# Decode attention inside a hybrid decoder step: three PSUM banks shared by turned keys and probabilities, and the splits of the value pages in another order

## The reference

```python
k_past = cache_k[l][page_table].reshape(n_dec, PAST_LEN, DA_HEADS, 2 * DA_HEAD_DIM)
v_past = cache_v[l][page_table].reshape(n_dec, PAST_LEN, DA_HEADS, DA_V_DIM)
k_all = jnp.concatenate([k_past, ka], axis=1)
v_all = jnp.concatenate([v_past, va], axis=1)
oa = diff_attention(qa, k_all, v_all, q_pos_s, k_pos_s, lam)

s = jnp.einsum('bqhmd,bkhmd->bhmqk', q, k) * (DA_HEAD_DIM ** -0.5)
p = jax.nn.softmax(s + bias, axis=-1)
a = p[:, :, 0] - lam * p[:, :, 1]
return jnp.einsum('bhqk,bkhd->bqhd', a, v)
```

## Time and profile before

| what | value |
|---|---|
| time, median of 3 runs | 1933.44 us (1932.71 to 1934.54) |
| time of the profiled execution | 1933.36 us |
| its span, first to last instruction | 1931.1 us |
| mean granted TensorE clock | 0.964 |
| PE busy over the span | 1776.0 us (92%) |
| DVE, ACT, POOL busy | 780.2 us (40%), 661.2 us (34%), 97.2 us (5%) |
| PE share of the chain that ended last | 85%, of which line 297 is 68% |

### The profile page before, as it was taken

How to read it: one execution, slowest core, us unless ns; L and a number is a source line. 1 busy time by engine, 2 the same in 40 slices (tenths; PEclk the granted TensorE clock), 3 DMA queues, 4 the chain that set the end, 5 groups by cost and what they waited for, 6 DMA issues and landing times.

```text
span 1931.1 us, 32243 instructions
## 1 busy us (share of the span) xinstructions
PE 1776.0 (92%) x13095; PEld 1678.0 (87%) x13095; DVE 780.2 (40%) x1084; ACT 661.2 (34%) x867; POOL 97.2 (5%) x169
## 2 busy tenths in 40 slices
PE   5999999998998775989889999899999899999996
PEld 5999999987997545777768999779998799999996
DVE  2333332244223775776753222344344433333123
ACT  3333331124223554666753222123322433332111
POOL 0000000000002420000000000210000000000002
PEclk9999999999998898999989999999999999999998
DMA  4222222230430014787851232152222122222221
GB/s 140 88 88 88 89 88 93 82 101 30 134 124 33 1 39 147 260 281 269 278 178 45 86 102 85 46 184 88 88 87 87 34 89 88 88 88 84 85 98 46
DMA packets 146734, 204.09 MB, mean 106 GB/s; under 512 B 5538, under 2 KB 127330, under 8 KB 146658
## 3 DMA queue, kind: packets, MB, share of 16 engines
q1 hardware_dynamic: 145506, 198.55, 31.6%
q0 software_dynamic: 1152, 4.46, 0.6%
HBM read 191.59 MB, written 11.40 MB: 105 GB/s over the span
## 4 chain that ended last, share of the span: by engine, by line
PE 85%; DVE 6%; ACT 5%; issue 3%; DMA 0%; SPq 0%; POOL 0%; POOLq 0%; ACTq 0%; DVEq 0%
PE ps L297 68%; PE ps L1255 3%; PE ps L1280 2%; PE ps L1237 2%; PE ps L974 2%; DVE vp_lo L1377 2%; ACT vp_hi L1373 1%; PE ps L988 1%; ACT kt_hi L1355 1%; PE ps L614 1%; PE ps L1683 1%; PE ps L1675 1%; PE ps L1295 1%; PE ps L699 1%; DVE kt_lo L1356 1%
## 5 line engine op out<-in xcount | busy, mean ns | idle before, releaser
L297 PE MATMUL ps<-xh,w_hi_t 128*128 128x272 f32 x2432 | 512.1, 292 | 27.4 <-DVE xl L651 18.6
L297 PE MATMUL ps<-xl,w_hi_t 128*128 128x272 f32 x2432 | 506.4, 290 | 0.0
L297 PE MATMUL ps<-xh,w_lo_t 128*128 128x272 f32 x2432 | 505.8, 290 | 0.0
L283 DVE TENSOR_TENSOR w_lo_t<-w_raw,w_hi_t 128x2048 fp32r<-128x2048 f32 (+1 forms) x112 | 252.4, 2254 | 519.2 <-ACT w_hi_t L279 519.2
L297 PEld LDWEIGHTS ps<-xh,w_hi_t 128*128 128x128 f32 x2432 | 385.6, 191 | 32.5 <-issue 21.1
L297 PEld LDWEIGHTS ps<-xl,w_hi_t 128*128 128x128 f32 x2432 | 386.7, 191 | 0.0
L297 PEld LDWEIGHTS ps<-xh,w_lo_t 128*128 128x128 f32 x2432 | 384.6, 191 | 0.0
L279 ACT CAST w_hi_t<-w_raw 128x2048 fp32r<-128x2048 f32 (+1 forms) x112 | 209.9, 1874 | 277.5 <-PE ps L297 277.5
L297 PE MATMUL ps<-hh,w_hi_t 128*128 128x272 f32 x704 | 145.8, 288 | 0.0
L297 PE MATMUL ps<-hl,w_hi_t 128*128 128x272 f32 x704 | 145.3, 288 | 0.0
L297 PE MATMUL ps<-hh,w_lo_t 128*128 128x272 f32 x704 | 144.9, 287 | 0.0
(11 more groups left out here) (243 smaller groups left out, 2040.4 us busy)
## 6 DMA issues: line engine op xcount, KB each, us to landing
w_raw<-in_ffn_w_gu_dram SPq DMA_DIRECT2D x44, 1024.0 KB, 5.0
w_raw<-in_w_in_dram SPq DMA_DIRECT2D x32, 1024.0 KB, 5.6
k_page<-in_cache_k_dram SPq DMA_DIRECT2D x64, 512.0 KB, 4.2
v_page<-in_cache_v_dram SPq DMA_DIRECT2D x64, 512.0 KB, 4.7
w_raw<-in_ffn_w_down_dram SPq DMA_DIRECT2D x16, 1024.0 KB, 5.1
w_raw<-in_ffn_w_down_dram SPq DMA_DIRECT2D x8, 768.0 KB, 4.4
w_raw<-in_w_branch_a_dram SPq DMA_DIRECT2D x4, 1024.0 KB, 5.1
st_in<-in_state_ret_dram SPq DMA_DIRECT2D x8, 512.0 KB, 5.3
```

The lines of the kernel that those rows point to most:

```text
L283: nc.vector.tensor_tensor(w_lo_t[:, j, 0:nk], w_raw[:, j, 0:nk], w_hi_t[:, j, 0:nk].bitcast(F32), ALU.subtract).then_inc(lo_split, 1)
L297: mm = nc.tensor.matmul(ps[:, bank + half, 0:HALF], w[:, j, k, w_cols], m[:, k0 + k, half * HALF:half * HALF + HALF], start=start and k == ...
```

## The change

Two things change, both inside `DecodeAttention`. The number and kind of instructions stays the same.

First, the turned key halves and the turned probabilities now go round three banks, 0, 1 and 5, in the order in which PE makes them: two halves for each key page, and the probabilities of request b-1 behind key page 2 of request b. Each of them waits until the work three places back has been read by DVE. Before, a key half waited for the half two places back.

Second, ACT and DVE take the value pages in another place: pages 2 and 3 right behind key page 3, and page g right behind key page g for g = 4 to 7. On ACT, key page 2 also goes ahead of the copy of the last output rows (`act_keep`). The order on PE, on POOL and on SP does not change.

```diff
+                order = []
+                for b in range(DEC):
+                    for g in range(PAGES):
+                        order += [("k", b, g, half) for half in range(2)]
+                        if b and g == 2:
+                            order.append(("p", b - 1))
+                order.append(("p", DEC - 1))
+                self.order = order
+                self.place = {item: n for n, item in enumerate(order)}
+
+            def bank(self, *item):
+                return (0, 1, 5)[self.place[item] % 3]
+
+            def bank_free(self, pe, *item):
+                n = self.place[item] - 3
+                if n >= 0 and self.order[n][0] == "k":
+                    _, b, g, half = self.order[n]
+                    pe.wait_ge(self.kT_lo, 16 * b + 2 * g + half + 3)
+                elif n >= 0:
+                    pe.wait_ge(self.pT_lo, 2 * self.order[n][1] + 3)
...
-                    pe.wait_ge(self.kT_lo, 16 * b + 2 * g + half + 1)
+                    self.bank_free(pe, "k", b, g, half)
                     for h in range(4):
-                        mm = nc.tensor.transpose(ps[:, half, h * P:h * P + P],
+                        mm = nc.tensor.transpose(ps[:, self.bank("k", b, g, half), h * P:h * P + P],
...
                 pe.wait_ge(self.pT_lo, 2 * b + 2)
-
-                nc.tensor.matmul(ps[:, 5, 0:ROWS], p_s[:, 0:P], ident[:, 0:ROWS], start=True, stop=True)
+                self.bank_free(pe, "p", b)
+                bank = self.bank("p", b)
+
+                nc.tensor.matmul(ps[:, bank, 0:ROWS], p_s[:, 0:P], ident[:, 0:ROWS], start=True, stop=True)
...
+                self.act_key(act, b, 2)
                 if older:
                     self.act_keep(act, b - 2)
-                self.act_key(act, b, 2)
...
                 self.act_key(act, b, 3)
+                if past:
+                    self.act_value(act, b - 1, 2)
+                    self.act_value(act, b - 1, 3)
                 for g in range(4, PAGES):
+                    self.act_key(act, b, g)
                     if past:
-                        self.act_value(act, b - 1, g - 2)
-                    self.act_key(act, b, g)
-                if past:
-                    self.act_value(act, b - 1, 6)
-                    self.act_value(act, b - 1, 7)
+                        self.act_value(act, b - 1, g)
...
                 self.dve_key(dve, b, 3)
+                if past:
+                    self.dve_value(dve, b - 1, 2)
+                    self.dve_value(dve, b - 1, 3)
                 for g in range(4, PAGES):
+                    self.dve_key(dve, b, g)
                     if past:
-                        self.dve_value(dve, b - 1, g - 2)
-                    self.dve_key(dve, b, g)
-                    if past and g == 5:
-                        self.dve_weigh(dve, b - 1)
-                if past:
-                    self.dve_value(dve, b - 1, 6)
-                    self.dve_value(dve, b - 1, 7)
+                        self.dve_value(dve, b - 1, g)
+                        if g == 5:
+                            self.dve_weigh(dve, b - 1)
```

More of the change, by code:

```diff
@@ L1261, in turn_p @@
                 pe.wait_ge(self.pT_lo, 2 * b + 2)
-                nc.tensor.matmul(ps[:, 5, 0:ROWS], p_s[:, 0:P], ident[:, 0:ROWS], start=True, stop=True)
+                self.bank_free(pe, "p", b)
+                bank = self.bank("p", b)
+                nc.tensor.matmul(ps[:, bank, 0:ROWS], p_s[:, 0:P], ident[:, 0:ROWS], start=True, stop=True)
                 for g in range(1, PAGES):
-                    nc.tensor.transpose(ps[:, 5, ROWS * g:ROWS * g + ROWS], p_s[0:ROWS, P * g:P * g + P],
+                    nc.tensor.transpose(ps[:, bank, ROWS * g:ROWS * g + ROWS], p_s[0:ROWS, P * g:P * g + P],
                                         ident[0:ROWS, 0:ROWS])
@@ L1349, in key_half @@
             def key_half(self, b, g, half, hi):
-                src = ps[:, half, :].rearrange("p (h c) -> p h c", c=P)
+                src = ps[:, self.bank("k", b, g, half), :].rearrange("p (h c) -> p h c", c=P)
                 n = slice(P * (g % 2), P * (g % 2) + P)
@@ L1378, in dve_value, with p_parts @@
                                         ).then_inc(self.v_lo, 1)
-            def p_parts(self):
-                return ((ps[:, 5, :].rearrange("p (g c) -> p g c", c=ROWS), pT[:, 0:PAGES, 0:ROWS],
+            def p_parts(self, b):
+                return ((ps[:, self.bank("p", b), :].rearrange("p (g c) -> p g c", c=ROWS), pT[:, 0:PAGES, 0:ROWS],
                          pT[:, 0:PAGES, ROWS:P]),
@@ L1413, in act_p @@
                 act.wait_ge(self.o_done, b + 1)
-                for src, hi, _ in self.p_parts():
+                for src, hi, _ in self.p_parts(b):
                     nc.scalar.copy(hi, src).then_inc(self.pT_hi, 1)
@@ L1494, in dve_p @@
                 dve.wait_ge(self.pT_hi, 2 * b + 2)
-                for src, hi, lo in self.p_parts():
+                for src, hi, lo in self.p_parts(b):
                     nc.vector.tensor_tensor(lo, src, hi.bitcast(F32), ALU.subtract).then_inc(self.pT_lo, 1)
```

## The result

| | before | after |
|---|---|---|
| median | 1933.44 us (1932.07 to 1934.96, 9 runs) | 1938.55 us (1936.33 to 1946.55, 9 runs) |
| profiled execution, its span | 1933.36 us, 1931.1 us | 1936.33 us, 1934.1 us |
| mean granted clock | 0.964 | 0.962 |
| first turn to last merge | 283.04 us | 287.59 us |

The ratio is 1.003 (95% interval 1.0019 to 1.004): the change made the kernel about 5.1 us slower. The forecast was 1940.0 us, slower by 6.6. The profiled execution is the fastest of the nine runs of the changed kernel, so the trace shows somewhat less than the median: 4.55 us within the decode stage, 0.93 us ahead of it and -2.5 us behind it.

A forecast was written before the change was run, and what follows sets the result against it. The decode attention stage was taken as bound by PE, broken by short waits. Terms 5.7 - 1.2 - 3.5 + 5.6 = +6.6 us on 1933.36 gave 1940.0 us, with a range from 1928 to 1949 us.

The forecast's parts named there:

- pairs: Key pages (4, 5) and (6, 7), seven requests: value split waits for `values`, each score 0.41 us late; +5.7 us.
- front of a request: Key page 1 to second score, six requests: third bank removes a half-turn wait, about 0.2 us gained each; -1.2 us.
- request 0, front of request 1: Turns with no values between: waits shrink or move earlier, scores wait for one subtraction less; -3.5 us together.
- falls of the clock: Waits of about 1.8 us ahead of late scores: four of 14 followed by 1.2 GHz, about 1.4 us each; +5.6 us.
- the old share: Four of seven waits from 1.46 us up in the old trace were followed by 1.2 GHz; forecast took 2 in 7.
- The rival with a holding clock: Decode stage: the clock stays full behind the long waits; 1934.4 us, no change that can be told; chance 0.27.
- That DVE work hangs on ACT's row of copies, the same number as before: Second score of a request: low part of key page 3 follows ACT's copies, so only about 0.2 us is gained.
- the bound of -4.9: Request 0 and front of request 1: largest gain, if the low-clock score at 756.10 becomes a fast one.
- The late value page: Value page 4's load may land after ACT wants it: nothing taken, upper bound 0.4 x 7 = 2.8 us.
- The rival that the bank was the limit: Front of a request: gain reaches the second score, 1.26 us in each of six requests; 1928.0 us; chance 0.18.

The follow-up runs named there:

- the filled kernel: The changed kernel with 12 unread turns of the identity ahead of each third and fourth score of requests 1 to 7, 168 in all: 1933.36 us.
- The order alone: The changed kernel with two banks for key halves and bank 5 for the probabilities, as before, keeping the new ACT and DVE order: 1940.21 us.
- the ring alone: The changed kernel with its three banks, but ACT and DVE in the order of before the change: 1925.65 us.
- the paired order: The changed kernel, three banks, with ACT and DVE taking key pages 4 and 5, then value pages 4 and 5, likewise 6 and 7: 1916.16 us.
- the copy put back: The changed kernel with ACT's copy of the finished output ahead of key page 2 again: 1937.65 us.

## Why the prediction was right

The time came out near the forecast, and by the mechanism forecast. All four terms have the sign that was forecast. The pairs have the size too; the front of a request was mis-sized by a wrong step, request 0 came out 1.0 us beyond its term, and the falls came near theirs partly by luck. All of it is taken from the profiled executions.

| term | predicted | measured | how |
|---|---|---|---|
| pairs | +5.7 | +5.6 | 6 x (0.41 + 0.39), and 0.39 + 0.42 in request 1 |
| front of a request | -1.2 | -2.4 | 6 x (-0.60 + 0.11 + 0.09) |
| request 0, front of request 1 | -3.5 | -4.5 | -5.73 + 1.19 |
| falls of the clock | +5.6 | +6.0 | 1.53 + 1.58 + 1.63 + 0.67 + 0.63 |
| sum | +6.6 | +4.7 | the stage is 4.55 longer |

**The pairs: right.** A delay of 0.41 us was read from one row of PE, the end of `values`, and the new rows have 0.41 from turn to score in the first pair; in the second the score is 7.73 - 7.34 = 0.39 later. (The request 1 entry is the filled kernel's 7.63 and 7.73 against 7.24 and 7.31 before, as there no fall mixes in.) ACT's split waits 0.29 us for `values`, not 0.4. The order alone has the delay, the ring alone has not, and when the paired order takes the value page from between the keys, the pair is shorter than before.

**The clock: right in kind, and in size partly by luck.** Five falls of 14, where four were forecast from four of seven waits in the old trace, each at 1.4 us; they average 1.2. That the old share was halved for the long work ahead of each wait has no run behind it: with the copy put back there are eight of 14, the old share without the halving, and the runs of the changed kernel spread from 1936.33 to 1946.55 us. One fall more and a lower price made up for each other. What the prediction didn't see is that the two places differ, 1.6 us behind a third score and 0.65 behind a fourth, where a wait of 0.75 us that was there anyway takes up a part. The rival with a holding clock had 1934.4 us; the filled kernel is that case, with 168 turns more, and took 1933.36. By the rule of the Trainium skill that the prediction weighed (TensorE: Matmul & The Clock Gate, HAM oscillation), the clock would have held, since the waits are shorter than the gaps that it names. Here it fell behind waits of 1.86 us, and held behind others of the same length.

**The front of a request: mis-sized.** The step that failed is "That DVE work hangs on ACT's row of copies, the same number as before". A row of the old trace, ACT, says otherwise:

```profile
901.27 1.08 ACT L1355 CAST kt_hi<-ps 128x512 fp32r<-128x512 f32 x2 [0.76 <-PE ps L1237]
```

ACT stood idle for 0.76 us ahead of key page 3, until PE had turned it. So that copy hung on PE, and behind it the DVE work that the earlier trace rows show at 901.89. When the first score came 0.60 us earlier, the turn behind it did, and ACT and DVE moved along. The rows of the changed kernel in request 4, PE:

```profile
864.10 0.60 PE L1259 MATMUL ps<-ident,k_page 128*128 128x128 f32 x4
865.45 0.66 PE L1259 MATMUL ps<-ident,k_page 128*128 128x128 f32 x4 [0.75 <-DVE kt_lo L1380]
...
869.10 0.39 PE L1274 MATMUL ps<-bias_r,ident_r 128*128 128x256 f32 x1
```

and DVE:

```profile
871.57 1.23 DVE L1401 TENSOR_TENSOR vp_lo<-v_page,vp_hi 128x1024 fp32r<-128x1024 f32 x1
872.71 1.28 DVE L1380 TENSOR_TENSOR kt_lo<-ps,kt_hi 128x512 fp32r<-128x512 f32 x2
```

The wait of 1.26 us is 0.75 now and lies between the halves of key page 1. DVE's low part of key page 3 ends at 873.99, and the second score starts at 874.05: here DVE's own row is the limit at last, value page 1 standing ahead of key page 3. The second score comes 0.60 - 0.11 = 0.49 us earlier. Because it starts behind a wait now, its second matmul follows the first by 0.23 us (905.73, 905.96 in request 5) in place of 0.12 (903.37, 903.49), and so the turn behind it stands 3.81 us from the score in place of 3.72. That 0.09 belongs here too; it is why the third score in the table is 0.50 later and the pair only 0.41. Of the 1.26 us per request 0.40 were gained in place of 0.2. The ring alone and the kernel with the copy put back both show the same first score, so the bank gives it, not the swap. The 0.11 is the swap's: with the copy put back the second score follows after 4.83 us again.

**Request 0: right in sign, beyond the size taken.** Its four scores in the changed kernel, PE (beside the earlier trace rows):

```profile
742.39 0.39 PE L1274 MATMUL ps<-bias_r,ident_r 128*128 128x256 f32 x1 [0.21 <-DVE kt_lo L1380]
...
747.11 0.39 PE L1274 MATMUL ps<-bias_r,ident_r 128*128 128x256 f32 x1 [1.56 <-DVE kt_lo L1380]
...
753.35 0.39 PE L1274 MATMUL ps<-bias_r,ident_r 128*128 128x256 f32 x1 [1.40 <-DVE kt_lo L1380]
...
759.57 0.59 PE L1274 MATMUL ps<-bias_r,ident_r 128*128 128x260 f32 x1 [1.40 <-DVE kt_lo L1380]
```

From the first turn (738.25) to the fourth score it takes 21.33 us in place of 27.06. The third score runs at full clock now, as the bound of -4.9 allowed; the first does so too, which it did not before (0.39 for its first matmul in place of 0.56) and which the prediction did not count. The fourth in turn runs at half clock, and of the 5.73 us the first two scores of request 1 give 1.19 back: 12.11 + 7.09 us against 11.47 + 6.54. The ring alone does the same (21.30, then 12.05 + 7.07).

**The late value page: right, nearly nothing.** One of them was late for ACT, in request 1:

```profile
782.95 1.05 ACT L1397 CAST vp_hi<-v_page 128x1024 fp32r<-128x1024 f32 x1 [0.39 <-DMA v_page<-in_cache_v_dram]
```

**The rival that the bank was the limit.** The bank does speed up the front, but by 0.6 us of the first score, not 1.26, and in the pairs by nothing. The rule of the Trainium skill beside it (Perfetto Trace Analysis, Optimization Strategy), that a recurring gap can mean too little PSUM, would have put the time at 1915.3 us. With the ring alone it is 1925.65, and its trace keeps about half of the 18.1 us:

```profile
PE ps L1259 <- DVE kt_lo L1380: 9.5, 11, 1.7
```

The paired kernel comes to 1916.16 us with the same 9.5 us of these waits, so it got there by shorter pairs and not by their going away.

So the change was two edits of opposite sign. The ring is worth some 7 us. The order costs about as much in late pairs (1940.21 us alone, against 1932.50 for before on the same chip), and on top of the ring it also gathers the waits of a pair into one, behind which the clock falls: from the ring alone to the changed kernel it is 12 to 13 us (1925.65 to 1938.55, less the 0.9 by which the kernels before differ), of which the late scores make 6.6 (6 x (0.12 + 0.45 + 0.40), and 0.81 in request 1) and the falls 6.0.

## What to carry to other kernels

When a step is put between two others on an in-order engine, ask which buffer it needs and when its last reader is done: here a split of value pages that could wait stood ahead of a key copy that could not, and some 0.4 us of it recurred 14 times. Before a stall is called the limit of the next row, read the bracket of each row in the chain behind it; a row with idle time of its own moves when its releaser moves. And test a change of two parts in its four combinations, since one part can hide a gain of the other.

## What was not expected of the hardware

Turns without use in a wait of PE made the kernel faster: 168 of them, 1.47 us for each 12, gave back 4 to 5 us, and the granted clock stayed at 1.00 where without them it fell to 0.50. The same late pairs with a wait in two pieces of 0.18 and 1.38 us had no fall, with one of 1.86 us five in one execution, and eight in an execution of nearly the same kernel.
